# Gate projection in pieces inside the first attention, an earlier first block, the spatial masks in eight parts, and another bank for MLA's fill

## The reference

```python
# first layer (gMLP): the spatial weights are masked, the gate is a projection
u, v, g = jnp.split(rms_norm(h) @ w_in, 3)          # 1024 -> 3 * 2048
wsm = jnp.where(tril, ws, 0)                        # 16 groups of 128 x 128
y = u * (einsum('gts,bcsgd->bctgd', wsm, layer_norm(v)) + bs) * silu(g)
h = h + y @ w_out
# second layer (sliding-window attention, 16 heads of 64, window 128)
q, g = jnp.split(rms_norm(h) @ w_in, 2)             # 1024 -> 2 * 1024
scores = q k^T / 8, masked;  m = max(scores, sink)
p = exp(scores - m) / (sum(exp(scores - m)) + exp(sink - m))
h = h + ((p @ v) * silu(g)) @ w_out
# later: retention, a PEER layer, MLA attention, a second PEER layer
c_q, c_kv, k_rope = split(h @ w_in)                 # MLA's first projection
```

## Time and profile before

| | us |
|---|---|
| median of 3 runs | 2379.41 (2378.58 to 2382.72) |
| the profiled execution | 2376.13 |
| its span in the profile | 2374.3 |
| TensorE busy in it | 2296.8 (97%) |
| VectorE busy | 1492.2 (63%) |
| ScalarE busy | 1166.0 (49%) |
| GpSimd busy | 1138.8 (48%) |

### The profile page before, as it was taken

How to read it: one execution, slowest core, us unless ns; L and a number is a source line. 1 busy time by engine, 2 the same in 40 slices (tenths; PEclk the granted TensorE clock), 3 DMA queues, 4 the chain that set the end, 5 groups by cost and what they waited for, 6 DMA issues and landing times. The chain is left out here.

```text
span 2374.3 us, 43154 instructions
## 1 busy us (share of the span) xinstructions
PE 2296.8 (97%) x13977; PEld 2045.4 (86%) x13977; DVE 1492.2 (63%) x3173; ACT 1166.0 (49%) x1775; POOL 1138.8 (48%) x493
## 2 busy tenths in 40 slices
PE   7999889999999999999999988899999999999998
PEld 5998868898999999988888877799999998888886
DVE  5433442332594888877777754429768886777777
ACT  5445434344455677743333334344557776333333
POOL 6868528576788666650000025368876667000000
PEclk9999999999999999999999999999999999999999
DMA  7544415445455444455556543245554445655653
GB/s 263 177 147 171 162 51 185 155 158 190 158 181 182 157 143 142 141 187 201 194 193 210 193 141 133 87 163 177 178 175 142 141 141 168 205 194 194 209 193 129
DMA packets 109593, 398.29 MB, mean 168 GB/s; under 512 B 12752, under 2 KB 13136, under 8 KB 108752
## 3 DMA queue, kind: packets, MB, share of 16 engines
q1 hardware_dynamic: 104688, 380.16, 47.9%
q10 hardware_dynamic: 4832, 17.17, 2.1%
HBM read 394.13 MB, written 3.15 MB: 167 GB/s over the span
## 5 line engine op out<-in xcount | busy, mean ns | idle before, releaser
L2031 POOL TENSOR_TENSOR w_lo<-ring,w_hi 128x1024 fp32r<-128x1024 f32 x474 | 1131.5, 2413 | 881.8 <-ACT w_hi L961 881.4
L961 ACT ACTIVATE w_hi<-ring 128x1024 fp32r<-128x1024 f32 x722 | 743.0, 1056 | 542.1 <-PE XX L435 389.4
L433 PE MATMUL GG<-hT_both,w_hi 128*128 128x256 f32 x1728 | 490.5, 284 | 3.4 <-POOL w_lo L2031 2.2
L434 PE MATMUL GG<-hT_both,w_hi 128*128 128x256 f32 x1728 | 488.9, 283 | 0.0
L435 PE MATMUL GG<-hT_both,w_lo 128*128 128x256 f32 x1728 | 488.9, 283 | 0.0
L543 PE MATMUL GG<-hT_both,w_hi 128*128 128x512 f32 x1152 | 410.4, 399 | 0.1
L433 PE MATMUL XX<-w_hi,hT_both 128*128 128x512 f32 x1024 | 398.8, 389 | 2.7 <-DVE w_lo L1897 2.1
L434 PE MATMUL XX<-w_lo,hT_both 128*128 128x512 f32 x1024 | 398.4, 389 | 0.0
L435 PE MATMUL XX<-w_hi,hT_both 128*128 128x512 f32 x1024 | 398.4, 389 | 0.0
L1897 DVE TENSOR_TENSOR w_lo<-ring,w_hi 128x1024 fp32r<-128x1024 f32 x248 | 303.9, 1225 | 56.1 <-ACT w_hi L961 56.0
L433 PEld LDWEIGHTS GG<-hT_both,w_hi 128*128 128x128 f32 x1728 | 331.5, 192 | 5.1 <-POOL w_lo L2031 2.6
(11 more groups left out here) (296 smaller groups left out, 2729.8 us busy)
## 6 DMA issues: line engine op xcount, KB each, us to landing
ring<-slabs_in SPq DMA_DIRECT2D x722, 512.0 KB, 4.0
big<-rows_in ACTq DMA_DIRECT2D x10, 512.0 KB, 7.0
big<-rows_in ACTq DMA_DIRECT2D x3, 1024.0 KB, 9.0
big<-keys_in ACTq DMA_DIRECT2D x2, 1024.0 KB, 7.6
h_kept<-h ACTq DMA_DIRECT2D x2, 1024.0 KB, 10.8
h<-h_kept ACTq DMA_DIRECT2D x2, 1024.0 KB, 6.7
big<-ws_in ACTq DMA_DIRECT2D x1, 1024.0 KB, 14.6
out<-h SPq DMA_DIRECT2D x4, 256.0 KB, 2.0
```

The source lines that it names most:

```text
L433: nc.tensor.matmul(out, a_hi, b_hi, start=start, stop=False, skip_group_check=True)
L434: nc.tensor.matmul(out, a_hi, b_lo, start=False, stop=False, skip_group_check=True)
L961: nc.scalar.activation(w_hi[:, 2 * j + half, :], ring[j][:, half * 1024:(half + 1) * 1024], ACT.Copy).then_inc(hi_ready, 1)
L2031: Q.tensor_tensor(w_lo[:, 2 * j + half, :], ring[j][:, half * 1024:(half + 1) * 1024], w_hi[:, 2 * j + half, :], ALU.subtract).then_inc(sp ...
```

## The change

The edits lie in four places of the program.

1. **Start.** ScalarE rounds block 0 before it splits the second half of slab 0 and before block 1's root; VectorE takes block 0's rest after block 1's variance, before its reciprocal. TensorE gets 22 matmuls of 128x128 that nobody reads before block 0's transposes and 13 behind them (`busy_at_start`, all into the bank of tile 2).
2. **Masks.** GpSimd masks the 16 spatial weights two at a time, after each of slabs 8 to 15; the attention's mask is made after the last. TensorE waits for all eight.
3. **First attention.** Only the gate's first slab is projected ahead. The other three are cut into 24 chunks of 6 matmuls (`gate_chunk`): four between and behind the transposes of q, and two ahead of the transposes of each of units 0 to 9. ScalarE splits the last gate slab and the first two of `b_out` (one half after the copies of units 0, 1, 3, 5, 7 and 9) and VectorE takes their rests, six instructions `w_lo<-ring,w_hi`, in place of GpSimd. ScalarE applies silu to the last three slabs behind the last exponentials. The products with the values move to the end: the first after unit 9, the third after unit 10, the second and fourth after unit 11.
4. **`b_out`** starts when the two values tiles of its first four rows of chunks are ready (`needed`), not all four.
5. **MLA's seam.** The fill writes 13 matmuls into `m_in`'s first G bank, not 14 into an X bank. MLA's own order of units stays.

```diff
+VALUES_OF = {"b": [range(0, 2), range(2, 4), range(4, 8), range(8, 12)], "m": [range(2 * i, 2 * i + 2) for i in range(4)]}
+VALUES_AT = {"b": {9: [0], 10: [2], 11: [1, 3]}, "m": {2: [0], 4: [1], 6: [2], 7: [3]}}
...
+            def busy_at_start(n):
+
+                for _ in range(n):
+                    nc.tensor.matmul(X[(X0["a_tr"] + 2) % 4][:, 0:P], ident[:, :], ident[:, :], start=True, stop=True)
+
             pe.wait_ge(sem("ident_ready"), 2)
+            busy_at_start(22)
             transpose_block("a_tr", xs, "xs_a", 0)
+            busy_at_start(13)
             block_taken("a_tr", 0)
...
-            pe.wait_ge(sem("ws_masked"), 1)
+            pe.wait_ge(sem("ws_masked"), 8)
...
-            project_cols("b_g", hT, DC)
+            project_slab(SLAB0["b_g"], 0, hT, DC, False)
+
+            def gate_chunk(n):
+
+                s, c = SLAB0["b_g"] + 1 + n // DC, n % DC
+                half = c // 4
+                if c == 0:
+                    bank_free(s, 0)
+                q = half_ready(s, 0, half)
+                for a in range(2):
+                    last = triple(G[s % 4][:, a * T:(a + 1) * T],
+                                  [x[:, q, (c % 4) * 256 + a * P:(c % 4) * 256 + (a + 1) * P] for x in (w_hi, w_lo)],
+                                  [x[:, c, :] for x in hT], c == 0 and a == 0, c == DC - 1)
+                if c % 4 == 3:
+                    last.then_inc(half_done, 1)
+
+            def gate_chunks(k):
+
+                for n in range(4 + 2 * k, min(6 + 2 * k, 3 * DC)):
+                    gate_chunk(n)
+
...
             pe.wait_ge(sem("q_rotated"), 4)
-            transpose_rows("b_qtr", B_q)
+            transpose_rows("b_qtr", B_q, tiles=(0, 1, 2))
+            gate_chunk(0)
+            gate_chunk(1)
+            transpose_rows("b_qtr", B_q, tiles=(3,))
+            gate_chunk(2)
+            gate_chunk(3)
...
-            attention("b", b_scores, b_transposes, b_values)
-            pe.wait_ge(sem("b_y_ready"), 4)
-            project_wide("b_out", (B_yh, B_yl))
+            attention("b", b_scores, b_transposes, b_values, gate_chunks)
+            project_wide("b_out", (B_yh, B_yl), sem("b_y_ready"), needed=lambda p, half: 2 * p + 2)
...
-            busy_until("m_tr", 2, 14)
+            bank_free(SLAB0["m_in"], 0)
+            keep_busy(G[SLAB0["m_in"] % 4], 13)
...
             split_half(0, 0)
-            root_block("a", 1)
-            split_half(0, 1)
             act.wait_ge(sem("cols_loaded"), 16)
             round_block("a_tr", hT_hi, 0, "a_g")
+            split_half(0, 1)
+            root_block("a", 1)
...
-            attention("b", True, DH ** -0.5)
+            attention("b", True, DH ** -0.5, then={
+                ("t", 0): lambda: split_half(SLAB0["b_g"] + 3, 0), ("t", 1): lambda: split_half(SLAB0["b_g"] + 3, 1),
+                ("t", 3): lambda: split_half(SLAB0["b_out"], 0), ("t", 5): lambda: split_half(SLAB0["b_out"], 1),
+                ("t", 7): lambda: split_half(SLAB0["b_out"] + 1, 0), ("s", 11): lambda: take_gates([1, 2]),
+                ("t", 9): last_gates})
...
+                if b == 1:
+                    dve.wait_ge(sem("cols_loaded"), 16)
+                    rest_block("a_tr", *hT, 0, "a_g")
...
-            g_read(dve, "b_g")
-            attention("b", True, DH ** -0.5, b_unit, b_gated)
+            dve.wait_ge(split_ready, 2 * (SLAB0["b_g"] + 3))
+            attention("b", True, DH ** -0.5, b_unit, b_gated, {10: [0], 11: [2, 1, 3]}, {
+                2: lambda: rest_half(SLAB0["b_g"] + 3, 0), 3: lambda: rest_half(SLAB0["b_g"] + 3, 1),
+                5: lambda: rest_half(SLAB0["b_out"], 0), 7: lambda: rest_half(SLAB0["b_out"], 1),
+                9: lambda: rest_half(SLAB0["b_out"] + 1, 0), 11: lambda: rest_half(SLAB0["b_out"] + 1, 1)})
...
-            Q.affine_select(out=A_ws, in_=A_ws, compare_op=ALU.is_ge, fill=0.0, base=0,
-                            pattern=[[0, 16], [1, P]], channel_multiplier=-1).then_inc(sem("ws_masked"), 1)
+            for q in range(8):
+                split(8 + q, 9 + q)
+                two = A_ws[:, 2 * q:2 * q + 2, :]
+                Q.affine_select(out=two, in_=two, compare_op=ALU.is_ge, fill=0.0, base=0,
+                                pattern=[[0, 2], [1, P]], channel_multiplier=-1).then_inc(sem("ws_masked"), 1)
```

More of the change, by code:

```diff
@@ L62, in attention_order @@
         out.append(("t", k))
-        while values < len(PV_AFTER[name]) and (PV_AFTER[name][values] < k or k == n - 1):
-            out.append(("v", values))
-            values += 1
+        out += [("v", i) for i in VALUES_AT[name].get(k, [])]
         if k + AHEAD < n:
@@ L447, in wide_half, with project_wide @@
                 return last
-            def project_wide(stage, src, ready=None, first=0):
+            def project_wide(stage, src, ready=None, first=0, needed=lambda p, half: 2 * p + half + 1):
                 per, groups = WIDE[stage], SLABS[stage] // WIDE[stage]
@@ L455, in inputs_ready @@
                     if ready is not None:
-                        pe.wait_ge(ready, 2 * p + half + 1)
+                        pe.wait_ge(ready, needed(p, half))
                 for g in range(first, groups):
@@ L602, in busy_until, with attention @@
                 keep_busy(x_begin(stage, i), n)
-            def attention(name, scores, transposes, values):
+            def attention(name, scores, transposes, values, between=None):
                 for kind, k in attention_order(name):
@@ L607, in attention @@
                     if kind == "t":
+                        if between is not None:
+                            between(k)
                         pe.wait_ge(sem(f"p_{name}"), k + 1)
                     if kind == "v":
-                        first = PV_AFTER[name][k - 1] + 1 if k else 0
-                        for u in range(first, PV_AFTER[name][k] + 1):
+                        for u in VALUES_OF[name][k]:
                             x_read(pe, f"{name}_t{u}")
@@ L1181, in _, with take_gates, last_gates @@
             take_T("b_qtr", B_qT)
-            attention("b", True, DH ** -0.5)
+            def take_gates(slabs):
+                for j in slabs:
+                    tile, free = g_tile(act, "b_g", j, j)
+                    nc.scalar.activation(flat(B_gT)[:, j * 512:(j + 1) * 512], tile[:, :], ACT.Silu).then_inc(free, 1)
+            def last_gates():
+                take_gates([3])
+                split_half(SLAB0["b_out"] + 1, 1)
+            attention("b", True, DH ** -0.5, then={
[3 more added lines that the diff above has]
+                ("t", 9): last_gates})
             seam("b_out", "fin", "r_v", lambda: round_block("r_tr", hT_hi, 0))
@@ L1502, in attention @@
                 maximum(1)
[L1503 to L1509, removed]
+                for k in range(UNITS[name]):
+                    normalize(k)
+                    if k + 2 < UNITS[name]:
+                        maximum(k + 2)
+                    if k in then:
+                        then[k]()
+                    for i in taken_at[k] if k in taken_at else []:
+                        take_values(i)
             hT = (hT_hi, hT_lo)
@@ L2063, in _ @@
                 pool.wait_ge(sem("pads_zero"), i + 1)
-            split(SLAB0["b_q"] + RING, SLAB0["v0"] + RING)
+            split(SLAB0["b_q"] + RING, SLAB0["b_g"] + 3)
+            pool.wait_ge(split_ready, 2 * (SLAB0["b_out"] + RING))
+            split(SLAB0["b_out"] + RING, SLAB0["v0"] + RING)
             pool.wait_ge(split_ready, 2 * SLAB0["m_in"])
```

25 lines of the change are left out of this document (15 added, 10 removed).

## The result

The changed kernel takes 2341.76 us (median of 4 runs, 2339.81 to 2343.09), the kernel before in the same set 2379.18; the ratio is 0.9839, with a 95% interval from 0.9822 to 0.9856. The profiled execution took 2341.94 us, its span is 2340.2 where it was 2374.3. Of the 34.1 us between the spans the first attention gave 24.4, more than the 20.4 I had put down; MLA took 2.5 back and what follows it 0.4, for which I had nothing. Between the medians lie 37.4 us: the profiled execution of the kernel before was 3.1 us under its median, that of the changed kernel stands at its own.

What follows compares the result with a forecast made beforehand. TensorE, busy 2296.8 of 2374.3 us, was taken as the bound, losing time to waits and low clock. Savings of 20.4 + 8.1 + 2.2 + 2.5 = 33.2 us gave 2342.9 to 2346.2, forecast 2345 us, range 2337 to 2355.

Steps and rivals of the forecast that it cites:

- first attention: From the gate's second slab to b_out: gate matmuls fill TensorE's waits, window falls to 54 us, 20.4 us saved.
- MLA's seam: Between block 0's and block 1's transposes in MLA: fill starts earlier, at the high clock, 8.1 us saved.
- masks: At slab 8: masks spread over eight slabs remove TensorE's whole wait for GpSimd, 2.2 us saved.
- start: Up to the first projections: earlier rounding and rest of block 0, TensorE's clock kept up, 2.5 us saved.
- The first rival: First attention stays bound by the chain from scores to probabilities: 12 us saved instead of 20.4, 2353 us; chance 18%.
- its own work is 1.76 us: First attention: TensorE's work per unit without waits; with 12 gate matmuls (1.44) it becomes 3.20 us.
- 57.06 - 5.75 / 2 = 54.2 us: First attention: the window's length if TensorE's work is packed without gaps and at 2.4 GHz.
- My bound of 21.5: First attention: upper bound of the saving, 21.5 us, if the drains of work cut by waits count in full.
- the 3.8 us: Start: saving if VectorE's two scalings of block 1 aren't held up by GpSimd's run, instead of 2.5 us.
- TensorE then probably runs at 2.4 GHz: Start: after the unread matmuls the first projections run at 2.4 GHz, where they ran at 1.2 before.
- Everything else keeps its order, so I carry each saving to the end unchanged: Whole kernel: savings at the four places reach the end in full, since what follows each place waits for TensorE.
- more is saved than I count: Rival: no drains in the attention, scalings at the start not held; 36 to 38 us saved, 2342 to 2338; chance 8%.

Runs made afterwards that it cites:

- e10: Changed kernel with each of VectorE's six rests in the first attention done twice: 2345.03 us, ratio 0.9857 to the kernel before.
- e2: Changed kernel with all four gate slabs projected ahead of the attention again, splits and rests in old places, values still at the end: 2350.63 us, ratio 0.9883.
- e3: Changed kernel with the whole first-attention part undone (gate ahead, values after units 1, 3, 7, 11, b_out waiting for all four tiles): 2364.31 us, ratio 0.9942.
- e5: Changed kernel with MLA's fill as before, 14 matmuls into an X bank: 2347.16 us, ratio 0.9867 to the kernel before.
- e8: Changed kernel with the single mask after slab 7 again and the attention's mask behind it: 2344.23 us, ratio 0.9859.
- e7: Changed kernel without the 22 and 13 unread matmuls at the start, new order kept: 2342.20 us, ratio 0.9847.
- e13: The changed kernel itself, run and profiled again unchanged in a later set: 2340.18 us, ratio 0.9845 to the kernel before.
- e6: Changed kernel with the start as before (roots and second half's split ahead of the rounding, no unread matmuls): 2344.97 us, ratio 0.9859.
- e4: Changed kernel with the attention's six rests given back from VectorE to GpSimd: 2346.12 us, ratio 0.9864 to the kernel before.

## Why the prediction was right, and where its sum was off

Predicted 2345 us in a range from 2337 to 2355, measured 2341.76. The terms of the sum, in us of the span:

| term | put down | measured | how |
|---|---|---|---|
| first attention | 20.4 | 24.4 | 74.43 - 50.08 |
| MLA's seam | 8.1 | 8.2 | 15.96 - 7.75 |
| masks | 2.2 | 2.2 | wait at `a_u` gone |
| start | 2.5 | 2.1 | 67.56 - 2.22 - 63.21 |
| the rest | 0 | -2.9 | 2.5 by the clock in MLA, 0.4 open |
| sum | 33.2 | 34.1 | 2374.3 - 2340.2 |

- **The mechanism in the attention held**: TensorE's work fills the units, PEclk is 1.00, PE 98% of the window, no wait at `b_out`, the waits for divisions all gone but one. The first rival is out; e10 shows the point from which it would decide.
- **The mis-sized step** is "its own work is 1.76 us" per unit, taken as 1.99 less the listed wait of 0.23. With no pause a unit is 2.96 us, and without its 12 gate matmuls 1.52. A listed wait of 0.23 us thus costs 0.46. I take it that a row's end includes the time until the last matmul has drained, and that this lies beside the next matmul only when there is one. The same made the packed window too long: "57.06 - 5.75 / 2 = 54.2 us" took the busy time for work, but packed, the work is 48.97, 5.2 less. The forecast of 54 us allowed two short waits (1.1 measured) and some 1.2 us for drains. Of the 5.2 us, 1.6 are the second stretch at the low clock, which the prediction passed over though the earlier trace rows point to it: PEclk 0.93 over 74.43 us is 0.07 x 74.43 x 2 = 10.4 us at 1.2 GHz, and the 6.8 are only two thirds of that. Whether the change or the moment removed this fall is open, since e2 lacks it and e3 has it behind the same waits. The other 3.6 us are the drains, 0.2 for each of the 18 pauses. My bound of 21.5 for them was too narrow. The Trainium skill (TensorE: Matmul & The Clock Gate, Single matmul latency) gives a single bf16 matmul at full clock (398 + N) / 2.4 ns; an estimate from that is some 0.17 us over its stream, and the 0.2 found per pause of these matmuls are near it.
- **I priced the wrong part as the main one.** The sum treated the filling by gate matmuls as the gain. Some 14.5 us of it come from the values at the end and the earlier `b_out` (e3 against e2), with what follows from them: no stop of VectorE, no low clock in the last units.
- **Seam, masks**: as put down, and their undoing in e5 and e8 brings the rows of before back.
- **Start**: held in its size. The two scalings took 2.4 us each, as feared, so the 3.8 us were out of reach here. That the 35 matmuls are of use was assumed with "TensorE then probably runs at 2.4 GHz"; it does, and e7 shows that nothing hangs on it, since GpSimd's halves set the pace to 21 us.
- **"Everything else keeps its order, so I carry each saving to the end unchanged"** failed for 2.9 us in the profiled execution. Order and waits were indeed unchanged, but the clock wasn't. Two errors of opposite sign, +4.0 and -2.9, brought the sum near in this pair of profiles, and that was luck: in e13 the -2.5 of MLA are not there.
- **By the medians** 37.4 us were saved where the sum has 33.2, so nothing made up for the 4.0 there. 2341.76 is the price of the rival to which I gave 8%, "more is saved than I count". Its "no drains" came true, "the scalings not held" did not. The forecast of 2345 stood 3.2 us off mainly by the drains and the second low stretch.

## What to carry to other kernels

When an engine waits in many units, look first at what its supplier does ahead of the late operation: a step in the supplier's queue that must itself wait (here a values tile ahead of a division) is cheaper to move than the gap is to fill. The move cured both attentions here, 14.5 us in one (with an earlier start of the next layer) and some 4 us of waits in the other. Count a wait of TensorE in short matmuls as its listed time plus a drain, and take the packed time from back-to-back spacing, never from the busy sum. Check the low stretches that you have found against PEclk of the whole window; here a third of the low time had been missed. Before handing VectorE's work to an idle GpSimd, see what else VectorE does at that time within SBUF; here six such hand-overs cost 4.5 us.

## What the runs showed of the hardware

- The same program with the same waits keeps TensorE's clock in one execution and loses it in another: behind a wait of 2.59 us PEclk is 0.56 in the changed kernel's first profile and 1.00 in its second. The same holds near 118 us, where TensorE waits 1.60 us for VectorE: behind it the next eight products take 1.75 us in e13, with PEclk 0.78 over the 3.0 us from 116.79, and behind the 1.59 us of the changed kernel's first profile 1.16 us, with 1.00; e6 and e10 fell there too. In e13 the way from `a_u` to `b_out` is 238.74 us for it, against 237.13. Each such fall costs 1.2 to 1.6 us, which is of the order of the scatter between runs (2339.08 to 2343.09).
- PEclk doesn't show the low speed at the very start. In e7 the projection's matmuls of 128x512 stand 0.43 us apart from 14.08 on, as at 1.2 GHz, in a window whose PEclk reads 1.00:

```profile
12.00:16.00 4.00, 2.48 (x6) 2.04 (x7) 3.96 (x9) 3.07 (x5) 2.84 (x2) 1.00 0.42 133
```

```profile
14.51 0.63 PE L434 MATMUL GG<-w_hi,hT_both 128*128 128x512 f32 x1
14.94 0.63 PE L432 MATMUL GG<-w_hi,hT_both 128*128 128x512 f32 x1
```

- GpSimd holds up VectorE even in an operation on 128x2 numbers within SBUF: 2.22 us instead of 0.16 (e4).
